# Transposes of two inputs and of the attention maps moved from TensorE to transfers and VectorE; norm rows in fp32r; FFN loop in another order

## What is computed

```
def forgetting_attention(q, k, v, logf):            # first block, 8 heads of 64
    c = cumsum(logf)
    for s0 in range(0, 256, 128):                   # two blocks ("tiles") of 128 queries
        s1 = s0 + 128
        logits = q[s0:s1] @ k[:s1].T * scale + c[s0:s1] - c[:s1]     # causal mask
        p = softmax(logits)
        out[s0:s1] = p @ v[:s1]

def first_block(x):
    proj = rmsnorm(x, norm_mix_pre) @ w_in          # q, k, v, f, g_b, g_c, hc, gate_conv, gate_attn
    ya = g_b * causal_depthwise_conv(g_c * hc, conv_w)
    yb = forgetting_attention(q, k, v, log_sigmoid(f + b_f))
    merged = sigmoid(gate_conv) * (ya @ w_branch[0]) + sigmoid(gate_attn) * (yb @ w_branch[1])
    x = x + rmsnorm(merged @ w_out, norm_mix_post)
    h = rmsnorm(x, norm_ffn_pre)
    g, u = split(h @ w_gate_up)
    return x + rmsnorm((silu(g) * u) @ w_down, norm_ffn_post)

def second_block(x, mem):
    # FFN, then retention + differential attention, memory attention, FFN, rmsnorm
    lam = exp(sum(lambda_q1 * lambda_k1)) - exp(sum(lambda_q2 * lambda_k2)) + lam_init
    kv = rms_norm(mem, norm_mem_kv) @ w_kv          # keys and values of the 256 memory rows
```

## Time and profile before

| quantity | us |
|---|---|
| time, median of 3 executions | 962.37 |
| the 3 executions | 962.37, 960.9, 962.5 |
| profiled execution | 960.9 |
| its span (first to last instruction) | 959.2 |
| PE busy | 950.1 (99% of the span) |
| DVE busy | 696.2 (73%) |
| ACT busy | 506.5 (53%) |
| POOL busy | 17.7 (2%) |
| share of the 16 DMA engines | 55.2% for the queue that carries nearly everything |

### The profile page before, as it was taken

The page is one execution under the profiler, slowest core; times in us unless marked ns, Lnnn a source line. Parts: engine busy times, 40 slices in busy tenths (PEclk is TensorE's granted clock), DMA queues, the critical chain, the costliest instruction groups (busy, mean ns, idle before and its releaser), DMA issues.

```text
span 959.2 us, 13255 instructions
## 1 busy us (share of the span) xinstructions
PE 950.1 (99%) x5128; PEld 820.0 (85%) x5128; DVE 696.2 (73%) x735; ACT 506.5 (53%) x695; POOL 17.7 (2%) x23
## 2 busy tenths in 40 slices
PE   9999999999999999999999999999999999999997
PEld 8887888888888888888888888899889888888886
DVE  5788768766776768877777676685776587767676
ACT  6535667754434345744343446574968554343433
POOL 0000000040000000000000000000000000000000
PEclk9999999999999999999999999999999999999999
DMA  9854595664555677555655554745445345556551
GB/s 310 243 180 137 203 276 193 201 208 164 194 182 182 209 203 219 192 176 176 216 177 200 185 184 140 227 140 176 169 139 197 132 133 185 210 176 218 175 175 44
DMA packets 138756, 178.49 MB, mean 186 GB/s; under 512 B 25867, under 2 KB 106205, under 8 KB 138589
## 3 DMA queue, kind: packets, MB, share of 16 engines
q1 hardware_dynamic: 138140, 175.60, 55.2%
q10 hardware_dynamic: 576, 2.36, 0.6%
HBM read 175.32 MB, written 1.05 MB: 184 GB/s over the span
## 4 chain that ended last, share of the span: by engine, by line
PE 97%; DVE 1%; ACT 1%; issue 1%; DVEq 0%; ACTq 0%
PE gate_banks L830 13%; PE up_banks L830 12%; PE bank L548 9%; PE bank L549 9%; PE bank L550 9%; PE up_banks L835 7%; PE gate_banks L835 7%; PE up_banks L548 7%; PE up_banks L550 6%; PE up_banks L549 6%; PE up_banks L673 2%; PE up_banks L676 1%; PE bank L731 1%; PE bank L960 0%; PE gate_banks L626 0%
## 5 line engine op out<-in xcount | busy, mean ns | idle before, releaser
L1836 DVE TENSOR_TENSOR w_lo<-stage,w_hi 128x2048 fp32r<-128x2048 f32 x81 | 185.4, 2289 | 96.5 <-ACT w_hi L1254 96.5
L1830 DVE TENSOR_TENSOR w_lo<-stage,w_hi 128x2048 fp32r<-128x2048 f32 x76 | 174.4, 2297 | 60.5 <-ACT w_hi L1247 60.2
L1247 ACT ACTIVATE w_hi<-stage 128x2048 fp32r<-128x2048 f32 x77 | 147.2, 1912 | 55.6 <-PE up_banks L676 22.3
L1254 ACT ACTIVATE w_hi<-stage 128x2048 fp32r<-128x2048 f32 x81 | 152.5, 1904 | 0.0
L830 PE MATMUL gate_banks<-act_both,w_hi 128*128 128x512 f32 x528 | 129.6, 391 | 0.0
L830 PE MATMUL up_banks<-act_both,w_hi 128*128 128x512 f32 x528 | 125.6, 390 | 0.0
L830 PEld LDWEIGHTS up_banks<-act_both,w_hi 128*128 128x128 f32 x528 | 98.7, 188 | 20.1
L830 PEld LDWEIGHTS gate_banks<-act_both,w_hi 128*128 128x128 f32 x528 | 95.7, 188 | 17.3
L1329 ACT ACTIVATE ffn_hi<-gate 128x512 fp32r<-128x512 f32 x30 | 19.0, 633 | 156.8 <-DVE gate L1968 156.8
L548 PE MATMUL bank<-w_hi,ffn_hi 128*128 128x512 f32 x240 | 93.8, 391 | 0.0
L549 PE MATMUL bank<-w_lo,ffn_hi 128*128 128x512 f32 x240 | 93.7, 391 | 0.0
(11 more groups left out here) (409 smaller groups left out, 1482.2 us busy)
## 6 DMA issues: line engine op xcount, KB each, us to landing
stage<-in_ffn_w SPq DMA_DIRECT2D x66, 1024.0 KB, 5.1
stage<-in_w_in SPq DMA_DIRECT2D x31, 1024.0 KB, 5.2
stage<-in_w_gate_up SPq DMA_DIRECT2D x22, 1024.0 KB, 5.1
stage<-in_w_down SPq DMA_DIRECT2D x11, 1024.0 KB, 4.9
stage<-in_w_out SPq DMA_DIRECT2D x8, 1024.0 KB, 4.8
stage<-in_mem_w_kv SPq DMA_DIRECT2D x8, 1024.0 KB, 5.1
stage<-in_w_branch SPq DMA_DIRECT2D x4, 1024.0 KB, 5.3
stage<-in_mem_w_q SPq DMA_DIRECT2D x4, 1024.0 KB, 4.9
```

Of the source, the lines that this page charges most:

```text
L1247: act.activation(w_hi[:, place, :], stage[:, place, :], copy).then_inc(hi_done, 1)
L1254: act.activation(w_hi[:, place, :], stage[:, place, :], copy).then_inc(hi_done, 1)
L1830: dve.tensor_tensor(w_lo[:, place, :], stage[:, place, :], w_hi[:, place, :].bitcast(F32), ALU.subtract).then_inc(lo_done, 1)
L1836: dve.tensor_tensor(w_lo[:, place, :], stage[:, place, :], w_hi[:, place, :].bitcast(F32), ALU.subtract).then_inc(lo_done, 1)
```

## The change

It has six parts.

1. The attention maps are no longer turned on PE. Their 32x32 blocks are moved by transfers of 128-byte pieces (`p_blocks`: 16 transfers per tile; of the second tile's, ten are issued by SP and six by ACT), and DVE turns each block (`turn_blocks`, two instructions for the first tile and four for the second). PE's products with v move one chunk later, and `keep_probs` falls away here.
2. The sums of `lam` are made on DVE from rows that are loaded to all partitions. PE's small matmul and the parameter rows that it used fall away.
3. The orders of ACT and DVE in this stretch are rewritten: `gate_in(GATE_C, 0, 1)` stands ahead of `exps(1)`, `normal(0)` ahead of `lo(14)`, and so on.
4. The diagonals are split into a high and a low part, so that `factor_rows` is two fp32r products of 256 columns with a ones matrix in fp32r.
5. The FFN loop goes by parts: high parts of gate and of up, low parts of gate and of up, then the down product. The chunks are loaded in the order gate, up, down. In the last FFN the factor rows move from the high part to the low part of the first up chunk.
6. The input of FFN0 is turned in the same way as the maps: 16 transfers (`x_blocks`, 12 from SP between the first and the second chunk of FFN0, 4 from ACT) and four DVE instructions, in place of `turn_x(S_FFN0)`.

The core of the diff, PE first:

```diff
-    for t in range(2):
-        mm = pe.matmul(bank[to][:, t * P:t * P + P], ones, diag[:, t, :], start=True, stop=True)
+    for x in (diag_hi, diag_lo):
+        mm = pe.matmul(bank[to][:, 0:T], ones_r[:, :], x.rearrange("p t q -> p (t q)"), start=x is diag_hi, stop=x is diag_lo)
...
     if ready is None:
         for m in range(2):
             for k in range(KD):
-                if second is not None and m == 0 and k == 2:
-                    second()
                 high(m, k)
         for m in range(2):
             for k in range(KD):
+                if late_rows is not None and m == 0 and k == 2:
+                    late_rows()
                 mm = low(m, k)
     else:
...
         c = base + 2 + t * 3
+        blocks = [(m, k) for m in range(2) for k in range(KD)]
+        pe.wait_ge(hi_done, c + 1)
+        pe.wait_ge(gate_read, t + (n + 1))
+        for m, k in blocks:
+            high_part(gate_banks, s[0], m, k)
+        pe.wait_ge(hi_done, c + 2)
+        pe.wait_ge(up_read, t + (n + 1))
+        for m, k in blocks:
+            high_part(up_banks, s[1], m, k)
         pe.wait_ge(lo_done, c + 1)
-        pe.wait_ge(gate_read, t + (n + 1))
-        halves_product(gate_banks, s[0])
+        for m, k in blocks:
+            mm = low_part(gate_banks, s[0], m, k)
+        mm.then_inc(used, 1)
+        pe.wait_ge(lo_done, c + 2)
+        for m, k in blocks:
+            mm = low_part(up_banks, s[1], m, k)
+        mm.then_inc(used, 1)
         if first:
             pe.wait_ge(rs_done, ROWS.index(norm) + 1)
-        ffn_chunk(c + 1, f, t, first, s[1])
-        pe.wait_ge(lo_done, c + 3)
-        pe.wait_ge(up_read, t + (n + 1))
-        halves_product(up_banks, s[2])
+        ffn_chunk(c + 2, f, t, first, s[2])
...
-pe.wait_ge(lg_free, 8)
-for e in range(2):
-    turn_probs(e, 0, lambda m: L0[:, m, :], 4 * e, 0)
-pe.wait_ge(par_ready, 2)
-pe.matmul(bank[SUM][:, 0:2], ones, lam_p, start=True, stop=True).then_inc(lam_done, 1)
 up_tok(GATE_C + 2, act_hi, act_lo, 1)
-for e in range(2, 6):
-    k0 = P * ((e - 2) // 2)
-    turn_probs(e, 1, lambda m: L1[:, m, k0:k0 + P], 4 * (e % 2), 0)
 up_tok(GATE_A, act_hi, act_lo, 0)
 up_tok(GATE_A, act_hi, act_lo, 1)
-pe.wait_ge(tp_free, 6)
+up_tok(GATE_A + 2, act_hi, act_lo, 0)
+pe.wait_ge(lg_free, 8)
+pe.wait_ge(p_turned, 6)
 for b in range(4):
     own = [slice(64 * i, 64 * i + 64) for i in range(2)]
     vs = [slice(b * P + 64 * i, b * P + 64 * i + 64) for i in range(2)]
     for i in range(2):
-        pe.matmul(pair[ACC + b][own[i], 0, :], v_tok[:, 0, vs[i]], p_T0[:, 2 * b + i, :],
+        pe.matmul(pair[ACC + b][own[i], 0, 0:P], v_tok[:, 0, vs[i]], p_a[:, 2 * b + i, :], start=True, stop=True)
+    for i in range(2):
+        pe.matmul(pair[ACC + b][own[i], 0, P:T], v_tok[:, 0, vs[i]], p_b[:, 4 * b + 2 * i, :],
                   start=True, stop=False)
     for i in range(2):
-        mm = pe.matmul(pair[ACC + b][own[i], 0, P:T], v_tok[:, 1, vs[i]], p_T1[:, 2 * b + i, :],
+        mm = pe.matmul(pair[ACC + b][own[i], 0, P:T], v_tok[:, 1, vs[i]], p_b[:, 4 * b + 2 * i + 1, :],
                        start=False, stop=True)
     mm.then_inc(pv_done, 1)
-up_tok(GATE_A + 2, act_hi, act_lo, 0)
 up_tok(GATE_A + 2, act_hi, act_lo, 1)
...
-turn_x(S_FFN0, 0)
-turn_x(S_FFN0, 1)
```

SP:

```diff
+def p_blocks(engine, tile, pieces):
+    L, to = ((L0, p_blocks0), (L1, p_blocks1))[tile]
+    from_ = L[:, :, :].rearrange("p a b -> p (a b)").rearrange("p (m k) -> p m k", k=P)
+    to = to.rearrange("p (m q) -> p m q", q=P)
+    for i in pieces:
+        q, r = slice(32 * (i // 4), 32 * (i // 4) + 32), slice(32 * (i % 4), 32 * (i % 4) + 32)
+        engine.dma_start(to[r, :, q], from_[q, :, r]).then_inc(p_landed[tile], 16)
+def x_blocks(engine, rows_):
+    for h in rows_:
+        tokens_ = slice(32 * h, 32 * h + 32)
+        for g in range(4):
+            r = slice(32 * g, 32 * g + 32)
+            engine.dma_start(v_flat.rearrange("p (a n) -> p a n", n=P)[r, :, tokens_],
+                             x_n[tokens_, :, :].rearrange("i t d -> i (t d)").rearrange("i (a f) -> i a f", f=P)[:, :, r]
+                             ).then_inc(x_blocks_landed, 16)
...
+    for c in range(GATE_C, GATE_A + 1):
+        gate_weights(c)
+    sp.wait_ge(negc_ready, 1)
+    sp.wait_ge(p_done, 1)
+    p_blocks(sp, 0, range(4))
+    gate_weights(GATE_A + 1)
+    p_blocks(sp, 0, range(4, 7))
+    gate_weights(GATE_A + 2)
+    p_blocks(sp, 0, range(7, 16))
+    gate_weights(GATE_A + 3)
+    sp.wait_ge(sel_done, 1)
+    sp.wait_ge(p_done, 2)
+    p_blocks(sp, 1, range(6))
+    first_branch_weights()
+    p_blocks(sp, 1, range(6, 10))
...
+    whole(FFN[0], a["w_gate_up"][0], 0, slot(FFN[0]))
+    sp.wait_ge(memt_turned, 4)
+    sp.wait_ge(x_done, 4 * S_FFN0 + 4)
+    x_blocks(sp, (0, 1, 2))
```

ACT and DVE:

```diff
 gate_in(GATE_C, 0, 0)
+gate_in(GATE_C, 0, 1)
+hi(16)
 exps(1, L1, T)
-gate_in(GATE_C, 0, 1)
...
 gate_in(GATE_C, 1, 0)
+act.wait_ge(sel_done, 1)
+act.wait_ge(p_done, 2)
+p_blocks(act, 1, range(10, 16))
 gate_in(GATE_C, 1, 1)
-for e in range(2, 4):
-    keep_probs(e, p_T0[:, 4 * e - 8:4 * e - 4, P:T])
-for e in range(4, 6):
-    keep_probs(e, p_T1[:, 4 * e - 16:4 * e - 12, :])
+hi(18)
 conv_hi(1)
-hi(18)
+gate_in(GATE_A, 0, 0)
+hi(19)
+gate_in(GATE_A, 0, 1)
+act.wait_ge(p_landed[1], 16 * 16)
+act.dma_start(mem_nat, a["mem_2"][0].rearrange("(t p) d -> p t d", p=P)).then_inc(mem_landed, 16)
+act.wait_ge(p_turned, 6)
+act.dma_start(table[:, :, :], a["consts"][:, C_END + 1024:C_END + 3072].rearrange("p (h m) -> p h m", h=8)
+              ).then_inc(table_landed, 16)
+hi(20)
 conv_hi(2)
 conv_hi(3)
...
     for t in range(2):
-        ins = dve.tensor_scalar(diag[:, t, :], ident, factors[n][:, t:t + 1], None, ALU.mult)
+        ins = dve.tensor_scalar(diag_hi[:, t, :], ident, factors[n][:, t:t + 1], None, ALU.mult)
+    then(ins)
+    for t in range(2):
+        ins = dve.scalar_tensor_tensor(diag_lo[:, t, :], ident, factors[n][:, t:t + 1], diag_hi[:, t, :].bitcast(F32),
+                                       ALU.mult, ALU.subtract)
     ins.then_inc(diag_done, 1)
...
 normal(0, L0, P)
+lo(14)
+lo(15)
+softmax_max(1, L1, T)
 conv(0)
 lo(16)
 normal(1, L1, T)
+lo(17)
+def turn_blocks(tile, of, to, n):
+    dve.wait_ge(p_landed[tile], 16 * 16)
+    for i in range(n):
+        dve.transpose(to[:, 512 * i:512 * i + 512], of[:, 512 * i:512 * i + 512]).then_inc(p_turned, 1)
+turn_blocks(0, p_blocks0, pa_flat, 2)
 conv_lo(0)
 conv(1)
-lo(17)
+lo(18)
 dve.wait_ge(lamx_done, 1)
 then(dve.tensor_tensor(lam, lam_e[:, 1:2], lam_e[:, 0:1], ALU.subtract))
 then(dve.tensor_scalar(lam, lam, -LAM_INIT, None, ALU.add))
+turn_blocks(1, p_blocks1, pb_flat, 4)
+lo(19)
 conv_lo(1)
 conv(2)
-lo(18)
 conv_lo(2)
 conv(3)
-lo(19)
 conv_lo(3)
 lo(20)
...
+dve.wait_ge(x_blocks_landed, 16 * 16)
+dve.wait_ge(mem_lo_done, 8)
+for part in (0, 2, 1, 3):
+    at = slice(512 * part, 512 * part + 512)
+    dve.transpose(k_flat[:, at], v_flat[:, at]).then_inc(x_blocks_turned, 1)
+for b in range(KD):
+    if b == 4:
+        lo(32)
+    dve.wait_ge(act_hi_done, 16 + b // 2 * 2 + 2)
+    dve.scalar_tensor_tensor(act_lo[:, b, :].rearrange("p (t n) -> p t n", t=2), x_T[:, :, b, :],
+                             par[:, G_FFN_PRE + b:G_FFN_PRE + b + 1],
+                             act_hi[:, b, :].bitcast(F32).rearrange("p (t n) -> p t n", t=2),
+                             ALU.mult, ALU.subtract).then_inc(act_lo_done, 1)
```

More of the change, by code:

```diff
@@ L257, in build @@
         x_turned, x_done = sem("x_turned"), sem("x_done")
+        lam_landed = sem("lam_landed")
+        p_landed, p_turned = [sem(f"p_landed{i}") for i in range(2)], sem("p_turned")
+        x_blocks_landed, x_blocks_turned = sem("x_blocks_landed"), sem("x_blocks_turned")
+        ones_ready = sem("ones_ready")
         act_hi_done, act_lo_done = sem("act_hi_done"), sem("act_lo_done")
@@ L409, in feed_forward @@
             def feed_forward(base, w_g, g_col, w_u, u_col, w_d, between=None):
-                whole(base, w_g, g_col, slot(base))
+                if base != FFN[0]:
+                    whole(base, w_g, g_col, slot(base))
                 whole(base + 1, w_u, u_col, slot(base + 1))
@@ L414, in feed_forward @@
                     whole(c, w_g, t * 256 + (g_col + 256), slot(base + 2))
-                    rows(c + 1, w_d, t * 256, 2, 0, D, slot(base + 3))
-                    whole(c + 2, w_u, t * 256 + (u_col + 256), slot(base + 4))
+                    whole(c + 1, w_u, t * 256 + (u_col + 256), slot(base + 3))
+                    rows(c + 2, w_d, t * 256, 2, 0, D, slot(base + 4))
                 last = base + FFN_CHUNKS - 1
@@ L459, in _, with first_branch_weights, gate_weights @@
                              ).then_inc(table_landed, 16)
+            def first_branch_weights():
+                rows(BR0, a["w_branch"][0, 0], 0, 4, 0, 512, slot(BR0))
             wholes(GB, w_in, 1544, 6)
-            for p in range(4):
-                token_pair(GATE_C + 2 * p, w_in, 3080 + 512 * p)
+            def gate_weights(c):
```

(21 more changed lines are left out.)

129 lines of the change are left out of this document (62 added, 67 removed).

## The result

The changed kernel is slower: 964.27 us (median of 7) against 961.07 of the kernel before (7), a ratio of 1.0027 with a 95% interval of 1.0015 to 1.0038. The profiled execution of the changed kernel took 964.13 (span 962.4, 3.2 more than the span before).

What follows compares the result with a forecast made beforehand. PE was taken to set the time, with waits of only 2.0 and 1.1 us. Terms -7.6 + 0.6 + 1.6 + 1.1 + 1.1 = -3.2 gave 957.7 against the profiled 960.9, 959.2 as a median; range 954.8 to 964.5.

Steps and rivals of the forecast that it cites:

- What leaves PE: On PE: gate-copy wait 2.0, turns of the maps 2.86, turn of FFN0's input 1.75, factor rows 1.0; 7.6 us saved.
- One, six issues on ACT: Second GATE_A stretch: six issues at 0.61 delay the fourth gate copy, so PE waits 0.6 us, bounds 0 and 1.4.
- Two, the branch weights: Turn of the merged rows: last branch weight late behind memory blocks, so PE waits 1.6 us, bounds 0 and 4.4.
- Three, `OUT1`: In OUT1: one lo on DVE ahead of four steps PE waits for, 1.1 us, bounds 0 and 2.2.
- Four, FFN0's start: FFN0's first product: SP's twelve issues, landing, turns and low parts end late; PE waits 1.1 us, bounds 0 and 2.5.
- The loop at zero: FFN loop by parts: the new order gains or loses nothing, 0 us with bounds -0.3 to 0.3.
- the sign of this fault: Inside the FFN loops: a new wait of PE would show the zero for the new order to be wrong.
- The diagonals: Factor rows as two 256-column fp32r products: 0.2 us saved at each of five places, 1.0 in all.
- the third: Rival: 64 KB transfers cost a queue more than 32 KB ones, up to +11.1 us (973.5) at double pitch; 13%.

Runs made afterwards that it cites:

- gate_copy_first: Changed kernel with the fourth gate copy and the last gate chunk's high part ahead of ACT's six issues; 962.44 us, 1.0005 of the kernel before.
- weights_first: Changed kernel with SP issuing the last two branch weights and first two OUT1 weights one group of eight memory blocks earlier; 959.64 us, 0.9974 of the kernel before.
- before_loop: Kernel before with the FFN loop by parts alone, the last FFN's factor rows in the low part; 963.38 us, ratio 1.0013.
- before_diagonals: Kernel before with the fp32r diagonals alone, the last FFN's rows staying in the high part; 961.98 us, ratio 0.9998.
- one_queue: Changed kernel with gate copy first, weights first and early first-up read, plus all sixteen second-tile transfers issued by SP; 959.36 us, 0.9973 of the kernel before.
- weights_behind: Changed kernel with gate copy first, weights first, early first-up read, and SP's ten second-tile transfers ahead of two weights; 955.78 us, 0.9939 of the kernel before.
- input_by_pe: Changed kernel with the turn of FFN0's input back on PE (part 6 undone); 964.51 us, 1.0025 of the kernel before.
- before_gate_copy: Kernel before with one edit, the second gate copy ahead of the second tile's exponentials on ACT; 958.75 us, ratio 0.9967.

## Why the prediction was wrong

The forecast was 3.2 us faster, with a range that just holds the result and a direction that does not. Step by step, against the profiled executions; where no wait or issue is named, a cost is how much later PE ends the same chunk than before, restarts included. (A chunk is 24 products of 512 columns or the like, 5.44 us on PE, not the 48 of the text ahead of the prediction; the forecast's 2.7 for half a chunk was right.)

- **What leaves PE (7.6): right.** It was 8.0: the wait was worth 2.3 with its restart, and the diagonals gave 0.2 at each of their five places. PE began the product that then waited 5.3 us earlier than before (105.2 against 107.69 + 2.8); the text had 5.1.
- **One, six issues on ACT (0.6): the step that failed.** It took 0.61 an issue from the earlier trace rows, where no 64 KB transfer stands behind a weight. They took 1.12. The copy came 3.0 late, and the 1.7 of the slow stretch behind it was no term at all. 4.9 in place of 0.6, outside the bound of 1.4. gate_copy_first takes these 4.9 away by moving the copy alone.
- **Two, the branch weights (1.6): 0.9, but by PE's own lateness.** The route was right: blocks, weight, high part, `merge(1)`. Its shift was 9.6 (115.79 to 125.35), not 5.6, since the maps were turned 2.7 later than assumed and `lo(19)` waited 1.06 for a high part that stands on ACT behind the late product. That the size came near is luck: gate_copy_first, where PE is earlier, waits 1.5 there.
- **Three, `OUT1` (1.1): 3.1, of which 2.4 are waits and the rest restarts. The second step that failed.** Named was a `lo` on DVE. It was the first `OUT1` weight, issued 7.6 us later than before, the shift that the last branch weight has against the earlier trace rows, with ACT's copies behind it. weights_first removes it by moving weights alone.
- **Four, FFN0's start (1.1): 1.6.** Right in place and near in size, by two errors that nearly cancel: the issues took 10.4 where 7.8 was said, and the last transfer landed 2.1 behind its issue where 3.5 was said.
- **The loop at zero: 1.3.** The text named such a wait as the sign of this fault, and before_loop shows it without the rest of the change. The working compared the passes of the loop with one another, not the first with the product ahead of it.
- **The diagonals (1.0): right on PE.** That before_diagonals shows no gain comes in part from its wait of 0.4, which the changed kernel does not have.

Sum: -8.0 + 4.9 + 0.9 + 3.1 + 1.6 + 1.3 = +3.8. The FFN loops, the new wait apart, are 0.5 shorter in all, which leaves +3.3, and the spans differ by 3.2. Of the 6.4 between forecast and result the gate copy makes 4.3, `OUT1` 2.0 and the loop 1.3; the other terms come to -1.1.

Of the rivals, the third was nearest: it had 64 KB transfers that cost more than 32 KB ones, at these three places. Its price was wrong. The extra is not the same for each transfer (0.63 to 0.65 in the median of one_queue and weights_behind); it lies in one or a few transfers of a group, and the 0.51 that an issue on ACT took more would have made +8.0 by its sum. Per byte even ACT's held group was not dear: 6.71 us for 384 KB, where twelve issues of 32 KB at 0.61 would take 7.3. It had 13%, where it deserved more: all its evidence for and against came from transfers that I had not seen in this company.

## What to carry to other kernels

Issues of transfers on a compute engine belong behind whatever another engine waits for: their length depends on what else is under way (6.71 us for ACT's six in the changed kernel, 4.4 in weights_behind). When a step is moved to transfers, ask which transfers now stand behind them in program order, and give the ones that feed the bound engine their place first; here swapping weights and blocks was worth 4.6 us, as much as all the transposes that left PE (2.86 + 1.75). Price a wait on the bound engine with its restart and with the slow clock that can follow.

## What the hardware showed unexpectedly

- SP's queue takes four 64 KB transfers of 128-byte pieces behind a 1 MB weight at 0.6 to 1.2 us each and holds the fifth for 1.9 to 2.8 us: so for the second tile in the changed kernel and in the seven others that issue it there. Without a weight just ahead the fifth is not held (weights_behind, where the third took 1.85), and the transfers of x lose as much in several steps as others in one. In the changed kernel ACT's queue, which carries no weights, was held at the same time. That fits what the Trainium skill says (DMA: Bandwidth & Descriptors, Issuing engines are not separate DMA queues), that transfers of all issuing engines share the same 16 DMA engines. The loss goes with a weight under way; what limits the number is open, and sizes between 32 and 64 KB were not tried.
- A wait of PE of 1.9 to 3.0 us can be followed by a stretch at 1.2 GHz that costs 1.5 to 1.7 us (the changed kernel, weights_first, gate_copy_first, one_queue), and 2.9 in input_by_pe. It need not be: the wait of 2.16 at 157.97 was not, nor the 2.0 in the profile of the kernel before. The kernel before shows the same in its times: of 23 executions 11 took 961.0 to 961.6 and 12 took 962.3 to 964.4, the first with a mean clock of 0.998 to 1.000 and the others of 0.996 to 0.997; with the 2.0 wait removed all five took 958.6 to 959.1. That is 2.4 below the first group, about the 2.3 of the wait with its restart, and the second group makes up the rest of before_gate_copy's 3.2. That the slow stretch makes the difference between the groups is argued from these numbers; no profile of that kernel has caught it.
